# Pair sums of the feed-forward's hidden blocks: both operands re-read from DRAM one tile later, summed in place

## The reference, cut to what matters

```python
# first block (phase E of the kernel), D_FF = 2816
h = rms_norm(x, norm_ffn_pre[l])
f = (jax.nn.silu(h @ w_ffn_gate[l]) * (h @ w_ffn_up[l])) @ w_ffn_down[l]
# second block (phase H), D_FF_2 = 2816, a convolution of width 3 along the tokens
h = x @ w_up
h = lax.conv_general_dilated(h, conv_w[:, None, :], window_strides=(1,),
    padding=[(CONV_WIDTH - 1, 0)], dimension_numbers=('NWC', 'WIO', 'NWC'),
    feature_group_count=h.shape[-1]) + conv_b
a, g = jnp.split(h, 2, axis=-1)
return (jax.nn.silu(g) * a) @ w_down
```

## Time and profile before

| what | value |
|---|---|
| median of three runs | 3157.57 us (3152.23 to 3159.49) |
| profiled execution, its own time | 3161.4 us |
| its span | 3159.7 us |
| PE / DVE / ACT / POOL busy | 93% / 60% / 42% / 23% of the span |
| granted TensorE clock, mean | 0.967 |

### The profile page before, as it was taken

The page is one execution under the profiler, slowest core; times in us unless marked ns, Lnnn a source line. Parts: engine busy times, 40 slices in busy tenths (PEclk is TensorE's granted clock), DMA queues, the critical chain, the costliest instruction groups (busy, mean ns, idle before and its releaser), DMA issues.

```text
span 3159.7 us, 41058 instructions
## 1 busy us (share of the span) xinstructions
PE 2939.5 (93%) x14905; PEld 2400.7 (76%) x14905; DVE 1897.9 (60%) x2684; ACT 1315.3 (42%) x2136; POOL 725.5 (23%) x645
## 2 busy tenths in 40 slices
PE   8989999999989798999999999999979899988898
PEld 6767778778868576788777887788867677767687
DVE  3546565565675647666556574555744776777656
ACT  3531441541542435233224453555644444333444
POOL 3211121221231301334662001333510000243200
PEclk8999999999999999999999999999989999999999
DMA  4256356356342562555458564557663344556765
GB/s 138 71 155 141 122 145 160 99 147 149 97 123 61 194 227 80 144 160 139 144 159 285 181 220 137 142 184 183 172 203 135 101 114 115 163 152 199 250 200 194
DMA packets 330037, 488.32 MB, mean 155 GB/s; under 512 B 18818, under 2 KB 214160, under 8 KB 329888
## 3 DMA queue, kind: packets, MB, share of 16 engines
q1 hardware_dynamic: 276064, 298.16, 30.3%
q0 software_dynamic: 48016, 171.37, 20.1%
q10 hardware_dynamic: 5808, 16.79, 1.8%
HBM read 379.24 MB, written 199.29 MB: 183 GB/s over the span
## 4 chain that ended last, share of the span: by engine, by line
PE 66%; DVE 13%; DMA 8%; ACT 6%; issue 3%; POOL 3%; SPq 1%; DVEq 0%; ACTq 0%; POOLq 0%
PE PS L671 19%; PE PS L2528 15%; PE PS L2548 12%; PE PS L377 5%; PE PS L1504 2%; DMA pair_hidden<-hidden_scratch 1%; DVE gate_up L2422 1%; PE PS L1470 1%; PE PS L1398 1%; DMA down_raw<-up_sums 1%; PE PS L1387 1%; DVE w_L L2374 1%; DMA sb_branch<-u_scratch 1%; PE PS L3218 1%; PE PS L3205 1%
## 5 line engine op out<-in xcount | busy, mean ns | idle before, releaser
L671 PE MATMUL PS<-hH,w_H 128*128 128x512 f32 x1072 | 453.5, 423 | 22.8 <-DVE w_L L334 12.5
L671 PE MATMUL PS<-hH,w_L 128*128 128x512 f32 x1072 | 426.2, 398 | 0.0
L671 PE MATMUL PS<-hL,w_H 128*128 128x512 f32 x1072 | 424.3, 396 | 0.0
L334 DVE TENSOR_TENSOR w_L<-w_raw,w_H 128x1024 fp32r<-128x1024 f32 x107 | 133.7, 1250 | 218.6 <-ACT w_H L329 218.4
L671 PEld LDWEIGHTS PS<-hH,w_H 128*128 128x128 f32 x1072 | 207.1, 193 | 68.4 <-issue 12.3
L2528 PE MATMUL PS<-hH,fast_w 128*128 128x512 f32 x672 | 232.6, 407 | 23.6 <-ACT gate_up L2300 21.2
L671 PEld LDWEIGHTS PS<-hH,w_L 128*128 128x128 f32 x1072 | 204.9, 191 | 46.6
L671 PEld LDWEIGHTS PS<-hL,w_H 128*128 128x128 f32 x1072 | 206.4, 193 | 35.8 <-issue 1.7
L2528 PE MATMUL PS<-sums,w_H 128*128 128x512 f32 x672 | 212.3, 398 | 8.4 <-DVE gate_up L2422 8.2
L2528 PEld LDWEIGHTS PS<-hH,fast_w 128*128 128x128 f32 x672 | 129.5, 193 | 61.8 <-ACT gate_up L2300 25.0
L2824 POOL TENSOR_SCALAR prob<-prob,den_inverse 128x128 f32<-128x128 f32 (+3 forms) x64 | 110.3, 1723 | 234.0 <-DVE den_inverse L3034 233.7
(11 more groups left out here) (477 smaller groups left out, 6758.6 us busy)
## 6 DMA issues: line engine op xcount, KB each, us to landing
up_sums<-in_w_up POOLq DMA_DIRECT2D x24, 1408.0 KB, 10.3
w_raw<-in_w_in SPq DMA_DIRECT2D x62, 512.0 KB, 4.6
u_scratch<-unit_staged SPq DMA_DIRECT2D x50, 512.5 KB, 5.2
hidden_scratch<-hidden SPq DMA_DIRECT2D x44, 512.0 KB, 5.0
pair_sums<-pair_sum POOLq DMA_DIRECT2D x22, 1024.0 KB, 5.6
turned_raw<-pair_sums SPq DMA_DIRECT2D x88, 256.0 KB, 3.0
turned_raw<-down_sums SPq DMA_DIRECT2D x88, 256.0 KB, 4.1
down_raw<-up_sums SPq DMA_DIRECT2D x42, 512.0 KB, 6.6
```

The lines of the kernel that those rows point to most:

```text
L334: e.tensor_tensor(wL[c % 2][:, :, :], raw[c % 2][:, :, :], f32(wH[c % 2][:, :, :]), ALU.subtract).then_inc(s_wL, 1)
L671: mm = e.matmul(PS[:, f.bank(o, half), :], w[:, k0 + k, :], x[:, k, half * HALF:(half + 1) * HALF], start=(k == 0 and j == 0), stop=(k == ...
```

## The change

Both hidden tiles of a pair are now loaded from DRAM, into `pair_sum` itself, and the four sums are made in place; `pair_hidden` is gone (its memory is a pad). Pair p is loaded at the end of POOL's turn t = 11 + p, behind the weight sums, and summed at the head of turn t + 1, ahead of the wait for that turn's weights. `hidden` is no longer read by POOL, so the two waits on `pair_summed` go. The sums end up at other indices, so the order in which the down product takes them changes. The slots of the down ring are filled in another order: step 5 takes the slot over the pad, step 13 the one over `hidden`, step 17 the one over `pair_sum`; steps 9 to 11 reuse the slots of steps 0 to 2. SP stores the last hidden tile after `down_load(11)` instead of after `down_load(8)`.

```diff
-        DOWN_A = ((HIDDEN, 0, 0), (HIDDEN, NG, 0), (SUMS, 1), (SUMS, 0), (SUMS, 3), (SUMS, 2), (HIDDEN, NG, 1))
+        DOWN_A = ((HIDDEN, 0, 0), (HIDDEN, NG, 0), (SUMS, 0), (SUMS, 3), (SUMS, 2), (SUMS, 1), (HIDDEN, NG, 1))
...
-        slot_no = lambda n: (0, 1, 2, NSLOT, NSLOT + 1)[n] if n < 5 else (n - 2) % NSLOT
+        SLOT_FIRST, SLOT_RING = (0, 1, 2, NSLOT, NSLOT + 1, 7, 3, 4, 5), (0, 1, 2, 7, 6, 3, 4, 5, 8)
+        slot_no = lambda n: SLOT_FIRST[n] if n < NSLOT else SLOT_RING[(n - NSLOT) % NSLOT]
...
-            if n == NG:
-                e.wait_ge(sem("fast_stored"), since(tag, "fast_stored", 16 * FT))
+            if n in (2 * NG - 2, 2 * NG - 1):
+                e.wait_ge(sem("fast_stored"), since(tag, "fast_stored", 16 * (n + 1)))
...
-            elif n in (5, 6):
+            elif n == 5:
+                e.wait_ge(sem("down_L"), since(tag, "down_L", 6))
+            elif n in (6, 7):
                 e.wait_ge(sem("fast_P"), since(tag, "fast_P", 7 * NW))
-            elif n == 7:
+            elif n == 8:
                 e.wait_ge(sem("hidden"), since(tag, "hidden", FT))
-            elif n == 8:
+            elif n == 13:
                 e.wait_ge(sem("fast_stored"), since(tag, "fast_stored", 16 * FT))
-                e.wait_ge(sem("pair_summed"), since(tag, "pair_summed", 8 * NG))
-            elif n == 9:
-                e.wait_ge(sem("pair_summed"), since(tag, "pair_summed", 8 * NG))
-                e.wait_ge(sem("down_L"), since(tag, "down_L", 6))
-            elif n == 10:
+            elif n == 17:
                 e.wait_ge(sem("pair_stored"), since(tag, "pair_stored", 16 * NG))
...
-                if n == 8:
+                if n == 11:
                     store(None, NW, FT - 1)
...
-            def pair_sums(it):
-                e.wait_ge(sem("hidden"), own("hidden", tag, 1, it, 1))
-                e.wait_ge(sem("pair_loaded"), since(tag, "pair_loaded", 16 * (it - NG) + 16))
-                if it > NG:
-                    e.wait_ge(sem("pair_stored"), since(tag, "pair_stored", 16 * (it - NG)))
+            def pair_sums(p):
+                e.wait_ge(sem("pair_loaded"), since(tag, "pair_loaded", 32 * p + 32))
...
-                e.tensor_tensor(s1, pair_h[:, hi], hfE[:, hi], ALU.subtract).then_inc(summed, 1)
+                a_lo, a_hi, b_lo, b_hi = (pair_sum[:, i, :] for i in range(4))
+                e.tensor_tensor(b_hi, a_hi, b_hi, ALU.subtract).then_inc(summed, 1)
                 done(1)
-                e.tensor_tensor(s2, pair_h[:, lo], s1, ALU.subtract).then_inc(summed, 1)
+                e.tensor_tensor(a_hi, a_lo, a_hi, ALU.subtract).then_inc(summed, 1)
                 done(2)
-                e.tensor_tensor(s4, hfE[:, lo], s2, ALU.subtract).then_inc(summed, 1)
-                e.tensor_tensor(s3, pair_h[:, lo], pair_h[:, hi], ALU.subtract).then_inc(summed, 1)
...
+                e.tensor_tensor(a_lo, a_lo, b_hi, ALU.subtract).then_inc(summed, 1)
+                done(3)
+                e.tensor_tensor(b_lo, b_lo, a_lo, ALU.subtract).then_inc(summed, 1)
...
-            def pair_load(it):
-                e.dma_start(pair_h[:, :], h_scr[:, it - NG, :]).then_inc(sem("pair_loaded"), 16)
+            def pair_load(p):
+                e.wait_ge(sem("fast_stored"), since(tag, "fast_stored", 16 * (NG + p + 1)))
+                if p:
+                    e.wait_ge(sem("pair_stored"), since(tag, "pair_stored", 16 * p))
+                for i in range(2):
+                    e.dma_start(pair_sum[:, 2 * i:2 * i + 2, :], h_scr[:, i * NG + p, :].rearrange("p (n c) -> p n c", n=2))\
+                        .then_inc(sem("pair_loaded"), 16)
...
             for t in range(NW):
+                if t > NG:
+                    pair_sums(t - NG - 1)
                 if t < NW - 1:
                     tile_loaded(t + 2)
...
-                if t == NG:
-                    e.wait_ge(sem("hidden"), since(tag, "hidden", 2))
                 if t > NG:
-                    pair_store(t - 1)
-                if t >= NG:
-                    pair_load(t)
+                    pair_store(t - NG - 1)
                 if tag == "E" and t < NW - 1:
                     weight_sums(1, t)
                 if t >= NG:
-                    pair_sums(t)
-            pair_store(NW - 1)
-            pair_load(NW)
-            pair_sums(NW)
-            pair_store(NW)
+                    pair_load(t - NG)
+            for p in range(NW - NG, NG):
+                pair_sums(p - 1)
+                pair_store(p - 1)
+                pair_load(p)
+            pair_sums(NG - 1)
+            pair_store(NG - 1)
...
             def up_start(c, it):
...
-                e.wait_ge(sem("pair_summed"), own("pair_summed", tag, 4 * c + 3, it, 4))
...
             def tile_hidden(c, it):
...
-                    e.wait_ge(sem("pair_summed"), own("pair_summed", tag, 4 * c + 3, it, 4))
```

More of the change, by code:

```diff
@@ L208, in build @@
                 ("down_H down_L", "EH", 2 * 7 * NG), ("down_used", "EH", 7 * NG - 6 - 6),
-                ("pair_loaded", "EH", 16 * NG), ("pair_summed", "EH", 8 * NG), ("pair_stored", "EH", 16 * NG),
+                ("pair_loaded", "EH", 32 * NG), ("pair_summed", "EH", 4 * NG), ("pair_stored", "EH", 16 * NG),
                 ("silu hidden", "EH", 1 + NW), ("y_part", "EH", 28), ("y_added", "EH", 20),
@@ L272, in build @@
                 op_pair = sb("down_operands_pair", [P, 8, HALF], F32R, s1)
-            pair_sum, pair_h, raw_first = T("pair_sum", (P, 4, HALF)), T("pair_hidden"), T("down_raw_first", (P, 2, HALF))
+            pair_sum, pad_E, raw_first = T("pair_sum", (P, 4, HALF)), T("pad_e"), T("down_raw_first", (P, 2, HALF))
             cvt = T("conv_columns", (P, 16))
@@ L2178, in pair_sums @@
                 summed = sem("pair_summed")
-                done = lambda n: e.wait_ge(summed, own("pair_summed", tag, n, it, 4))
-                s1, s2, s3, s4 = (pair_sum[:, i, :] for i in range(4))
-                e.tensor_tensor(s1, pair_h[:, hi], hfE[:, hi], ALU.subtract).then_inc(summed, 1)
+                done = lambda n: e.wait_ge(summed, since(tag, "pair_summed", 4 * p + n))
+                a_lo, a_hi, b_lo, b_hi = (pair_sum[:, i, :] for i in range(4))
+                e.tensor_tensor(b_hi, a_hi, b_hi, ALU.subtract).then_inc(summed, 1)
@@ L2182, in pair_sums @@
                 done(1)
-                e.tensor_tensor(s2, pair_h[:, lo], s1, ALU.subtract).then_inc(summed, 1)
+                e.tensor_tensor(a_hi, a_lo, a_hi, ALU.subtract).then_inc(summed, 1)
                 done(2)
-                e.tensor_tensor(s4, hfE[:, lo], s2, ALU.subtract).then_inc(summed, 1)
-                e.tensor_tensor(s3, pair_h[:, lo], pair_h[:, hi], ALU.subtract).then_inc(summed, 1)
-            def pair_store(it):
-                e.wait_ge(sem("pair_summed"), since(tag, "pair_summed", 4 * it + 4))
-                e.dma_start(pair_scr[:, :, it - NG, :].rearrange("n p c -> p n c"), pair_sum[:, :, :])\
-                    .then_inc(sem("pair_stored"), 16)
@@ L2193, in pair_load, with pair_store @@
-            def pair_load(it):
-                e.dma_start(pair_h[:, :], h_scr[:, it - NG, :]).then_inc(sem("pair_loaded"), 16)
+                e.tensor_tensor(a_lo, a_lo, b_hi, ALU.subtract).then_inc(summed, 1)
+                done(3)
+                e.tensor_tensor(b_lo, b_lo, a_lo, ALU.subtract).then_inc(summed, 1)
+            def pair_store(p):
+                e.wait_ge(sem("pair_summed"), since(tag, "pair_summed", 4 * p + 4))
+                e.dma_start(pair_scr[:, :, p, :].rearrange("n p c -> p n c"), pair_sum[:, :, :])\
+                    .then_inc(sem("pair_stored"), 16)
@@ L2199, in tile_loaded @@
                     e.wait_ge(sem("fast_T"), since(tag, "fast_T", 32 * j))
-            e.sem_inc(sem("pair_summed"), 4 * NG)
             if tag == "E":
```

## The result

| | before | changed |
|---|---|---|
| median | 3159.31 us (5 runs) | 3138.04 us (3128.74 to 3140.25, 5 runs) |
| ratio | 1 | 0.9931, 95% interval 0.9914 to 0.9948 |
| span of the profiled execution | 3159.7 us | 3136.3 us |

21 us faster, where 51.5 were forecast; 3138 lies above the range of 3092 to 3125.

A forecast was written before the change was run, and what follows sets the result against it. PE takes two thirds of the chain, and pair work lengthens loop turns and leaves waits behind them. Gains 10 + 23.5 + 7 + 11 = 51.5 us, from 3157.6 to 3106; 8-in-10 range 3092 to 3125.

The forecast's parts named there:

- H's loop: Phase H's turns with pair work: both waits go, gaining 23.5 us (17 to 27.5).
- The cost of the waits: H's loop: all of 219.0 - 191.5 = 27.5 us comes back if the turn returns to 20.05 us.
- The collisions: H's loop: sums some 13 us after landing may cost the second tap 0.92 us a turn, 8 us; half taken.
- E's loop: Phase E's turns with pair work: load and pair sums leave the critical stretches, gaining 10 us (3 to 15).
- POOL's round of 19.8 us: E's loop: POOL's closed round of store, weight sums, loads and pair sums sets the turn; 3 us lost.
- Behind the loops: Down product's steps after both loops: gaps before step 11 close; 7 us in E, 11 in H.
- ACT would reach step 16: Behind both loops: ACT gets there 24.6 us after step 0, before step 11 is due at 30.2.
- The wait at step 17: Behind the loops: new wait for the last pair's store, held in time by 10 us in E, 2 in H.
- Rival 1: Half-gain: POOL's sums collide with H's taps every turn and E's round is 20.7 us; 39 us gained, 3119; 15%.
- taps on `hidden` of 2.2 us: H's loop: sign in the profile after that would show rival 1.
- Rivals 2 and 3: 2: step 17 waits 5 to 10 us for a store, 3119, 12%; 3: slow pair loads in E, 3152, 6%.
- Rival 4: Both loops: turns stay at 21.3 and 23.1 us because something else sets them; only the ends gain, 3140; 3%.

The follow-up runs named there:

- Run 2: Kernel before without the pair sums of pairs 1 to 10 in each phase, loads, stores and waits kept; 3111.85 us, ratio 0.9823.
- run 5: Changed kernel with H's sums held for DVE's first product sum and E's for the turn's last low part; 3118.48 us, ratio 0.9862.

## Why the prediction was wrong

**H's loop: this is the step that failed.** 23.5 us forecast, none measured, and that is most of the 30 us by which the sum was too high. Two terms were wrong.

*The cost of the waits, 27.5 us.* The prediction took the whole surplus of H's turns as the price of ACT's wait for the third pair sum, since the chain showed a DMA of 6.05 us behind it. The trace of the kernel before has the price: ACT's timeline in a turn without and in one with pair work, and DVE's operations ahead of it.

```profile
2703.35 1.24 ACT L2276 ACTIVATE hidden<-gate_up,conv_columns 128x1024 f32<-128x1024 f32 x1 [2.97 <-DVE gate_up L2422]
...
2748.98 1.24 ACT L2276 ACTIVATE hidden<-gate_up,conv_columns 128x1024 f32<-128x1024 f32 x1 [5.37 <-POOL pair_sum L2185]
...
2743.90 2.20 DVE L2404 SCALAR_TENSOR_TENSOR silu_out<-gate_up,conv_columns,silu_out 128x1022 f32<-128x1022 f32 x1
2746.03 1.78 DVE L2374 TENSOR_TENSOR w_L<-down_raw,w_H 128x512 fp32r<-128x512 f32 x1
2747.74 0.68 DVE L2422 TENSOR_TENSOR gate_up<-PS,gate_up 128x512 f32<-128x512 f32 x1
```

ACT's idle time grows by 5.37 - 2.97 = 2.40 us. Of these 0.92 + 1.10 = 2.02 are the gate tap and the low part on DVE, which the pair sums stretched in the kernel before as well; ACT needs DVE's fifth sum behind them in any case. The wait for POOL adds only the other 0.38, and in three of the nine turns DVE's sum came after POOL's and it added nothing. The same row of the changed kernel:

```profile
2753.07 1.24 ACT L2277 ACTIVATE hidden<-gate_up,conv_columns 128x1024 f32<-128x1024 f32 x1 [4.91 <-DVE gate_up L2421]
```

There 4.91 us stand against 2.89 in a turn without sums: 2.02 again. So the change took away a wait of some 0.4 us a turn and left the collisions; with the sums starting 11.0 us after the weights instead of 7.7, the first hidden tap took 1.91 us where it had taken 1.45. Run 2 agrees: without the sums, and with the waiting for the load kept, the turn is 20.03 us.

*The collisions, 4 us.* The prediction saw that the sums would meet DVE's taps, put their start 13 us after the weights, gave the meeting one tap of 0.92 us and charged half of that. The start was 11.0 us: the rows it used were those of a store and a load in flight together; apart the store took 4.6 us instead of 5.6 and the second load 4.8 instead of 6.05. Two microseconds earlier lie the gate tap, the low part and the first hidden tap, 2.65 us in the turn shown, and PE's idle time brought the clock down besides. A landing time was taken as if a late value were the cautious one; for a collision no value is cautious, and the whole turn of DVE should have been laid beside the sums.

**E's loop: 10 us forecast, 9.4 measured, in part by luck.** That the pair sums leave the two `low`s held. But the 3 us that were taken off were put down to POOL's round of 19.8 us, and the turns came at 20.0 for another reason: in most turns the first sum ran beside the last low part (1.58 us instead of 0.68 in the turn shown), which leads to the next weights. Holding the sums back sets POOL's round back, and yet it gave 19.5 (run 5).

**Behind the loops: 18 forecast, 10 measured** (5.4 + 5.0, with the other phases between E's step 0 and H's turns in the first). The copy behind step 16 was named as what starts step 11, and that held. What failed is that ACT would reach step 16 at 24.6 us after step 0: its split ended 32.8 us (E) and 37.0 us (H) after it. In E the loads of steps 6, 11 and 15 ahead of it took 7.2, 5.9 and 8.7 us, and the sums of pair 9 stretched the low parts (5.96 us for four, which take 2.5 undisturbed). The residual loads had moved away, but the pair loads and the later store of the last tile had moved in; what each of them cost was not separated. Without sums step 11 is on time in E even with the copy behind step 16 (30.1), in H it still comes at 33.7. The wait at step 17, the new one, had been placed right: ACT waited 9.0 us there in E, and PE did not stand for it.

**The rivals.** Rival 1 (collisions, 3119) had the right mechanism for H, and its sign, taps on `hidden` of 2.2 us, is there in six of nine turns; but it counted 10.5 of the loop's 27.5 us as lost, where all were. Rivals 2 and 3 did not occur: PE did not stand at step 17, and the pair loads took at most 4.8 us in the loops and 8.8 behind them. Rival 4 (3140) came nearest in time and had H's turns right, which stayed at 23.1; E's turns, which it also held fixed, did shorten, and what set H's was not a load but the sums. The Trainium skill's rule of a port held for a whole instruction (SBUF — State Buffer, section "SBUF: two separate sides") would have given 1.3 us a tap. In H's pair turns of the changed kernel the increases are 0.16 to 1.10 us for one operation, none of a whole sum. That each meets a sum already under way would explain it; no run separates that. Several operations a turn are hit, which the rule allows and which the prediction did not count.

## What to carry to other kernels

A wait in the chain is worth only what the engine would not have waited anyway: look for the other operand it needs (here 0.4 us of an idle time of 5.4) before the whole surplus is booked as gain. When a wait between two engines is removed, ask what the released work will run beside, and lay the whole turn of the other engine next to it; work that nobody waits for can still set the pace. If such work must run, hold it back for the moment at which the chain passes to an engine that it does not disturb: here one added wait gained 0.6%. And where one copy frees a bank for the next product, place it behind the last operand that is needed before it, not behind the lookahead.

## What was not expected of the hardware

A POOL store of 1024 KB landed in 4.6 us alone and in 5.6 us with a 512 KB load issued behind it. Beside POOL's additions a copy of 128 x 8 on DVE took 1.00 us instead of 0.17, and low parts of 128 x 512 up to 1.79 us instead of 0.68 in H and up to 2.28 in E, where POOL's weight sums run as well, while DVE's sums with one input in PSUM stayed at 0.67 to 0.69 us in both loops of every run.
